# Hybrid encoder block on one core: block 0 in two tiles, and the second expert choice moved beside block 1's projections

## The reference

```python
proj = h @ w_in                                   # GDN q,k,v,z,a,b | FoX q,k,v,f | two merge gates
y_a = _gdn_branch(...)                            # conv + SiLU, L2 norm, chunked delta rule, gated RMS norm
y_b = _fox_branch(...)                            # 8 heads of causal attention with forget gates
mix = jax.nn.sigmoid(gate_a) * y_a + jax.nn.sigmoid(gate_b) * y_b
h = _layernorm(DEEPNORM_ALPHA * h + mix @ w_o, ln1_g, ln1_b)
...
top_s, top_i = lax.top_k(scores, PEER_TOPK)       # per head: 2 x 128 scores, 16 best of each
best_s, best_pos = lax.top_k(cand.reshape(...), PEER_TOPK)
u = jnp.take(u_tab, e_blk, axis=0)                # 8 x 16 = 128 rows of 1024 for every token
act = jax.nn.gelu(jnp.einsum('td,tkd->tk', h_blk, u), approximate=False) * g_blk
vv = jnp.take(v_tab, e_blk, axis=0)
y = jnp.einsum('tk,tkd->td', act, vv)
h = _layernorm(DEEPNORM_ALPHA * h + y, ln2_g, ln2_b)
```

## Time and profile before

| | |
|---|---|
| median of 3 executions | 3630.0 us (3629.85 to 3632.14) |
| the profiled execution | 3634.61 us |
| its span, first to last instruction | 3632.9 us |
| mean granted TensorE clock | 0.812 |
| busy: PE, DVE, POOL, ACT | 68%, 58%, 62%, 18% of the span |
| moved by DMA | 1290.18 MB, mean 355 GB/s |
| of it, expert rows | 1073.87 MB |
| chain that ended last | PE 25%, DMA 24%, POOL 17%, DVE 15%, issue 13% |

### The profile page before, as it was taken

How to read it: one execution, slowest core, us unless ns; L and a number is a source line. 1 busy time by engine, 2 the same in 40 slices (tenths; PEclk the granted TensorE clock), 3 DMA queues, 4 the chain that set the end, 5 groups by cost and what they waited for, 6 DMA issues and landing times.

```text
span 3632.9 us, 37417 instructions
## 1 busy us (share of the span) xinstructions
PE 2487.4 (68%) x12216; PEld 1529.5 (42%) x12216; DVE 2100.5 (58%) x4943; ACT 659.0 (18%) x1657; POOL 2243.1 (62%) x2093
## 2 busy tenths in 40 slices
PE   8888994676976876666977877667796730133355
PEld 6676772444744543433745543434563410000010
DVE  5133799885468776455359776455447569744400
ACT  3331321332013212322003312321101000000000
POOL 1000477677537766677566766677766667777774
PEclk9999997887998988877988988867798875555676
DMA  5214799899979999999999999999999999999997
GB/s 174 84 61 157 290 404 369 312 370 377 412 283 375 409 403 370 328 384 385 411 412 351 409 406 389 332 386 391 383 414 381 409 409 409 410 409 409 409 410 317
DMA packets 367626, 1290.18 MB, mean 355 GB/s; under 512 B 39596, under 2 KB 68148, under 8 KB 362308
## 3 DMA queue, kind: packets, MB, share of 16 engines
q0 software_dynamic: 294912, 1073.87, 75.8%
q1 hardware_dynamic: 66760, 201.33, 14.9%
q10 hardware_dynamic: 5760, 12.59, 0.9%
HBM read 1274.65 MB, written 12.98 MB: 354 GB/s over the span
## 4 chain that ended last, share of the span: by engine, by line
PE 25%; DMA 24%; POOL 17%; DVE 15%; issue 13%; ACT 3%; DVEq 2%; SPq 0%; ACTq 0%; POOLq 0%
DMA ring<-in_ev,idxT 11%; PE banks L1507 10%; POOL ring L788 9%; DVE ring L1203 7%; POOL ring L774 7%; DMA ring<-in_eu,eidx 5%; PE banks L1517 5%; PE banks L1496 4%; DMA arena<-in_eu,eidx 4%; PE banks L1780 2%; DMA arena<-in_ev,idxT 2%; PE banks L1636 1%; POOL arena L788 1%; DMA arena<-d_rows 1%; PE banks L1558 1%
## 5 line engine op out<-in xcount | busy, mean ns | idle before, releaser
L774 POOL DMA_INDIRECT ring<-in_eu,eidx x938 | 1058.4, 1128 | 898.6 <-DVE eidx L1466 436.4
L788 POOL DMA_INDIRECT ring<-in_ev,idxT x894 | 971.0, 1086 | 368.1 <-issue 251.7
L1203 DVE CUSTOM_DVE_ANT_0 ring<-ring,h_cur 128x1024 f32<-128x1024 f32 x768 | 906.7, 1222 | 188.6 <-DMA ring<-in_eu,eidx 186.3
L1496 PE MATMUL banks<-ring,wide 128*32 128x512 f32 x3576 | 642.0, 800 | 509.5 <-DMA ring<-in_ev,idxT 436.8
L1507 PE MATMUL banks<-arena,wslot 128*128 128x256 f32 (+1 forms) x3248 | 751.1, 389 | 16.4 <-DMA wslot<-in_w_pq 9.5
L1507 PEld LDWEIGHTS banks<-arena,wslot 128*128 128x128 f32 (+1 forms) x3248 | 624.5, 195 | 176.2 <-issue 68.8
L1496 PEld LDWEIGHTS banks<-ring,wide 128*32 128x32 f32 x3576 | 120.4, 131 | 839.1 <-DMA ring<-in_ev,idxT 437.2
L1203 DVE CUSTOM_DVE_ANT_0 ring<-ring,banks 128x1024 f32<-128x1024 f32 x170 | 205.7, 1221 | 109.1 <-DMA ring<-in_eu,eidx 105.8
L1517 PE MATMUL banks<-arena 128*128 128x128 f32 x1408 | 210.7, 307 | 35.6 <-ACT arena L957 33.6
L1517 PEld LDWEIGHTS banks<-arena 128*128 128x128 f32 x1408 | 198.9, 219 | 78.4 <-ACT arena L957 43.5
L1496 PE MATMUL banks<-arena,wide 128*32 128x512 f32 x520 | 143.7, 900 | 112.0 <-DMA ring<-in_ev,idxT 60.6
(11 more groups left out here) (294 smaller groups left out, 2844.0 us busy)
## 6 DMA issues: line engine op xcount, KB each, us to landing
wslot<-in_w_pq SPq DMA_DIRECT2D x64, 576.0 KB, 8.2
wslot<-in_w_mix SPq DMA_DIRECT2D x24, 1536.0 KB, 10.6
wslot<-in_w_qkv SPq DMA_DIRECT2D x48, 512.0 KB, 7.4
wslot<-in_w_fqk SPq DMA_DIRECT2D x32, 512.0 KB, 8.2
wslot<-in_w_out SPq DMA_DIRECT2D x8, 2048.0 KB, 10.8
ring<-in_eu,eidx POOLq DMA_INDIRECT x938, 13.6
ring<-in_ev,idxT POOLq DMA_INDIRECT x894
wslot<-in_w_z SPq DMA_DIRECT2D x16, 512.0 KB, 7.0
```

What stands on the lines that cost most here:

```text
L774: pool.indirect_dma_start(out=place(UPOS[k]), out_offset=None, in_=eu, in_offset=bass.IndirectOffsetOnAxis(ap=eidx[:, n % (2 * TT), c // T ...
L788: pool.indirect_dma_start(out=place(VPOS[k]), out_offset=None, in_=ev, in_offset=bass.IndirectOffsetOnAxis(ap=idxT[:, n % (2 * TT), t:t + ...
L1203: dve.tensor_tensor_reduce(out=row, in0=row, in1=h_cur[:, n % 3, :] if n < NT - TT else hp[n % 2], scale=1.0, scalar=0.0, op0=ALU.mult, op ...
L1496: last = pe.matmul(BY[k][32 * j:32 * j + 32, :], wide32[:, at:at + 32], place(VPOS[4 * q + j])[:, k * 512:(k + 1) * 512], start=(m == 0), ...
```

## The change

- Block 0 goes tile by tile. First come the projections, chunk 0 and the gates; then tile 0's own 9 attention units, `ot`, 8 `mix` on 128 tokens, 2 `wo`, `ln` and its choice. Chunk 1 and tile 1's attention and merge (`delta_of(1) + attend_of(1) + merge_of(1)`) are spread among the first choice.
- The second choice comes after that, with block 1's projections spread among it; its scores are computed anew for tile 1 (queries by 128x128 matmuls; `kept` is gone).
- Block 1's delta rule has no other units beside it.
- `mo`, `w_out` and `w_pq` weights are fetched once per tile of block 0. The second tile's two halves of `w_out` share one half of `wslot`, so the second is fetched when the first has been used.
- SP issues the decays of chunk 1 at the first level of chunk 0 instead of after the last, in all blocks.
- In block 0, DVE adds the identity at each level; the identity matmul and ACT's copy are gone there.
- Four ring slots hold block 0's data until the first choice is done (`LENT`). `SECOND, VSECOND` become 208, 96.

What `pace()` asks for at the borders of the stages (U items / V items done):

| by the unit | before | changed |
|---|---|---|
| `idx 0` of block 0 (end of the first choice) | 106 / 0 | 106 / 0 |
| `idx 1` of block 0 (end of the second choice) | 160 / 64 | 177 / 68 |
| block 1's attention begins | 162 / 64 | 209 / 96 |
| block 1's merge begins | 211 / 92 | 255 / 116 |
| block 1's first head is chosen | 256 / 120 | 256 / 120 |
| block 2's merge begins | 461 / 324 | 485 / 348 |
| block 3's layer norm | 768 / 632 | 768 / 628 |

```diff
-SECOND, VSECOND = 160, 64
+LENT = [11, 12, 15, 16]
+SECOND, VSECOND = 208, 96
...
+def delta_of(c):
+    return [("prod", c)] + [("lev", LEVELS * c + l) for l in range(LEVELS)] + [("wu", c), ("ws", c), ("o", c), ("og", c)]
...
+def attend_of(t):
+    return [u for m in range(FH + 1) for u in (("att", (FH + 1) * t + m), ("ato", (FH + 1) * t + m))] + [("ot", t)]
...
+def merge_of(t):
+    return [("mix", PH * t + i) for i in range(8)] + [("wo", TT * t + nh) for nh in range(2)] + [("ln", t)]
...
-    beside = [u for u in PROJECT if u not in early] + [u for m in range(MA + 1) for u in (("att", m), ("ato", m))]
+    beside = [u for u in PROJECT if u not in early]
...
+        if kind == "lev" and i or kind in ("ws", "o", "og"):
+            units += [("gt", 0, m), ("gt", 0, m + 1)]
+            m += 2
+    units += [(kind, 0, i) for kind, i in attend_of(0) + merge_of(0)]
+    units += [(kind, 0, i) for kind, i in spaced(PASSES[0], delta_of(1) + attend_of(1) + merge_of(1), 2)]
     for b in range(NB):
         if b:
-            late, done = PASSES[1][:-1] if b == 1 else [], 0
-            for n, (kind, i) in enumerate(DELTA[:-1]):
...
+            units += [(kind, b, i) for kind, i in DELTA[:-1] + ATTEND[:1] + DELTA[-1:] + ATTEND[1:] + MERGE]
         after = PROJECT if b + 1 < NB else []
-        choose = CHOOSE if b else PASSES[0]
+        choose = CHOOSE if b else PASSES[1]
...
     if name in ("mix", "wo"):
-        return n % 2, 0, 24 * P if name == "mix" else 32 * P
+        return 1 if n >= 2 and name == "wo" else n % 2, 0, 24 * P if name == "mix" else 32 * P
...
             def lev(b, cl):
+                c, l = divmod(cl, LEVELS)
+                if l == 0 and c + 1 < TT:
+                    sp.wait_ge(g["exps"], TT * b + c + 1)
+                    sp.wait_ge(g["qk"], TT * b + c + 1)
+                    gates(TT * b + c + 1)
...
-            def wu(b, c):
-                if c + 1 < TT:
-                    sp.wait_ge(g["wu"], TT * b + c + 1)
-                    gates(TT * b + c + 1)
...
+            def first_block(t):
+                W, KH, VH = P * (t + 1), KH0[t], VH0[t]
...
+                else:
+                    sp.wait_ge(g["S"], TT)
+                    sp.wait_ge(g["oT"], TT)
+                for i in range(FH // 2):
+                    row = FOX0 + 2 * i
+                    sp.dma_start(KH[0:FD, i, :, 0:W], d_fk[i, :, 0:W].rearrange("(j p) w -> p j w", j=2)).then_inc(s_att[i % 2], 16)
...
             def wo(b, i):
                 nh, tt = divmod(i, TT)
+                if b == 0:
+                    sp.wait_ge(s_nat, i + 1)
...
+                    elif i == 2:
+                        fetch("wo", 3)
...
+                if n == 1:
+                    dve.wait_ge(s_hTe, 1)
+                    dve.wait_ge(s_h1st, 16)
...
+                if b == 0:
+                    dve.wait_ge(g["lp"], n * LEVELS + l + 1)
+                    dve.tensor_tensor(Pm, ident[:, None, :].to_broadcast([P, GH, P]),
+                                      B[4][:, :].rearrange("p (a b) -> p a b", a=GH), ALU.add).then_inc(g["lpe"], 1)
...
-                pe.matmul(B[4][:, :], ident[:, :], ident[:, None, :].to_broadcast([P, GH, P]), start=True, stop=False)
+                if b:
+                    pe.matmul(B[4][:, :], ident[:, :], ident[:, None, :].to_broadcast([P, GH, P]), start=True, stop=False)
```

More of the change, by code:

```diff
@@ L53, with spaced @@
 CHOOSE = [u for i in range(PH) for u in (("top", 2 * i), ("top", 2 * i + 1), ("cand", i), ("sel", i))] + [("idx", 0)]
+def delta_of(c):
[4 more added lines that the diff above has]
+    return [("mix", PH * t + i) for i in range(8)] + [("wo", TT * t + nh) for nh in range(2)] + [("ln", t)]
+def spaced(main, beside, ahead):
+    out, done = [], 0
+    for n, u in enumerate(main):
+        out.append(u)
+        upto = min(len(beside), max(0, (n + 1 - ahead) * len(beside) // (len(main) - 2 * ahead)))
+        out += beside[done:upto]
+        done = max(done, upto)
+    return out + beside[done:]
 def order():
@@ L212, in slots @@
         held[n] = p
-    return slot, before, wide
+    return slot, before, wide, full
 WEIGHED = [s - 1 for s in BEGUN]
-SLOT, BEFORE, WIDE = slots()
+SLOT, BEFORE, WIDE, FULL = slots()
 PLACED = UNITS.index(("idx", NB - 1, 0)) + 1
@@ L674, in wo @@
                 nh, tt = divmod(i, TT)
+                if b == 0:
+                    sp.wait_ge(s_nat, i + 1)
+                    if i == 0:
+                        for n in range(3):
+                            fetch("pq", n)
+                    elif i == 1:
+                        for n in range(4):
+                            fetch("mo", PH + n)
+                    elif i == 2:
+                        fetch("wo", 3)
+                    else:
+                        for item in range(4):
+                            fetch(*PITEMS[item])
+                    return
                 if tt == TT - 1:
@@ L1651, in wu @@
                 pe.wait_ge(g["kbg"], n + 1)
-                if b == 0 and c == TT - 1:
+                if b == 0 and c == 0:
                     pe.wait_ge(s_sga[0], 3)
@@ new lines, in att0, with ato0 @@
+                if last_n is not None:
+                    r = last_n % 2
+                    pe.wait_ge(s_ex[r], last_n // 2 + 1)
+                    pe.wait_ge(s_Oe, last_n)
+                    for k in range(t + 1):
+                        last = pe.transpose(TB0[t][:, k * P:(k + 1) * P], SX0[t][:, r, k * P:(k + 1) * P], ident[:, :])
+                    last.then_inc(s_T, 1)
+            def ato0(u):
+                t = u // (FH + 1)
+                n = step(0, u)[1]
+                if n is not None:
+                    i, j, _ = head_of(0, n)
+                    pe.wait_ge(s_Te, n + 1)
+                    for k in range(t + 1):
+                        last = pe.matmul(TB0[t][:, 0:FD], PT0[t][:, k, :], VH0[t][:, i, k, FD * j:FD * (j + 1)],
+                                         start=(k == 0), stop=(k == t))
+                    last.then_inc(s_O, 1)
@@ L1772, in wo @@
                 nh, tt = divmod(i, TT)
+                if b == 0:
+                    t, nh = divmod(i, TT)
+                    for j in range(2):
+                        pe.wait_ge(s_mix[j], 4 * (t + 1))
+                    arrived(b, "wo", i)
+                    pe.wait_ge(s_natev[nh], 2 + t)
+                    w = item("wo", i, KB)
+                    for k in range(KB):
+                        last = pe.matmul(B[4 + nh][:, :], MIXT[t][:, k, :], w[:, k, :], start=(k == 0), stop=(k == KB - 1))
+                    last.then_inc(s_nat, 1)
+                    return
                 if i == 0:
                     for j in range(2):
-                        pe.wait_ge(s_mix[j], 4 * (b + 1))
+                        pe.wait_ge(s_mix[j], 4 * (b + 2))
                 arrived(b, "wo", nh)
```

433 lines of the change are left out of this document (297 added, 136 removed).

## The result

The changed kernel takes 3795.3 us (median of 5 runs, 3789.4 to 3805.2) where the kernel before takes 3632.1 beside it (5 runs). The ratio is 1.0443, with an interval of 1.0421 to 1.0465: slower, by 163 us. Predicted were 3765 us and a range of 3670 to 3830. The profiled execution took 3805.2 us, its span is 3803.5; the forecast made against the profiled time was 3772.

What follows compares the result with a forecast made beforehand. PE was taken to bound the kernel before the first gather and DMA most stages after; stages summed to 1235 us against 1083.7, taken as +145, then -8: 3772 us profiled, 3765 median, range 3670 to 3830.

Steps and rivals of the forecast that it cites:

- The sum up to block 1's first gather: All stages up to block 1's first chosen head: 1235 us against 1083.7, 151 us later, of which 145 was taken.
- A: Start to the first gather: 324 us where 394.6 stood, a gain of 70, between 60 and 85.
- B: First choice, with tile 1's work beside it: 289 us against 197.9, ends 244 and 310; DMA cannot fill it.
- C: Second choice with block 1's projections: set by DMA, 245 us, ends 232 and 265.
- rival 3: Second choice: POOL's issue bounds it at 2.29 us per gather, 73 us more, time 3838; chance 0.08.
- D: Block 1's delta rule alone: a chain of 125 us, ends 105 and 140.
- E to G: Block 1's attention 92 us, merge to first query 128, then to the first head 32.
- rival 1: DMA bounds every stage, so only bytes and the earlier start count: 3629 or about 3600 us, not slower; chance 0.12.
- rival 2: Better overlap in first choice (250 us) and lone delta rule (115), both late waits won: 3700 to 3720 us; chance 0.25.
- The sum behind it: All after block 1's first head is chosen: decays' gain against a dry spell, tail the same, net -8 us.
- the dry spell: Block 2's `wo` to the next choice: items done sooner leave it without gathers, costing 10 to 20 us.
- up to 28 us come back: Delta rules of blocks 2 and 3: earlier decays remove waits of 14.17 and 14.56 us in stages with idle DMA.

Runs made afterwards that it cites:

- the second group: Runs on the quick chip: the changed kernel, 3804.0 us, and the same with SECOND, VSECOND = 160, 64, 3749.6 us, beside the kernel before, 3630.3 us.

## Why the prediction was right, and where not

**The sum up to block 1's first gather** held: 133 us later, where 151 was worked out and 145 taken. Part of that is luck, since its terms were off by -10, -22, +7, +12 and -6 us, and these cancel in part.
- A, to the first gather: 314 against 324 forecast. The gain is 81, not 70. From the merge on, PE's pieces came as said: the merge 31 to 16 us, the output projection 27.70 to 14.20.
- B, the first choice: 267 against 289. DVE was busy for 201 us, not the 229 summed: this is the term that was off. It did 98 U items there and not 106, which is 9 us; the rest isn't split. What DVE was to stand came as summed, 66 us against 60. The waits were there: 18.9 us for the output weight against 22 by the landing time of the earlier trace rows, 14.1 for the levels against 18. By the Trainium skill's page "DMA: Bandwidth & Descriptors", section "Anatomy of one DMA — SWDGE (gpsimd) path", the estimate was 14; that section is about transfers that POOL issues, while SP issues these, and the measured value lies between the two. The wait for tile 1's keys, put at "a few us", was 20.4.
- C, the second choice with the projections: 252 against 245, at DMA share 1.01 as forecast. POOL was busy for 177.60 us with 152 gathers, 1.17 each, so rival 3 (2.29 each) did not come. The earlier trace rows call DVE idle beside the gather of 0.94 us at 414.10; it was not, it ran short sorting operations there (0.09 to 0.69 us), and U items of 1.22 us beside the gather of 1.99. So what goes with the longer gathers is that kind of DVE work.
- D, the delta rule alone: 137.5 against 125. C + D is 390 where 370 was forecast and 201.7 stood: the largest loss, as predicted, and the thick delta rules show its kind.
- E to G, attention to the first head: 246 against 252.
B, C and D together are 657 us, forecast 659, where rival 1 needed 515. By the bytes that did move in them (75, 99 and 41 MB at 409 GB/s) it would have been 527, so rival 1 is out by either count. Rival 2 (B 250, D 115) did not come either.

**The sum behind it failed**: -8 forecast, +37.6 measured. The mis-sized term is "the new pace does block 2's items sooner and stands dry from its `wo` to the next choice, which costs 10 to 20". I took the dry spell for a small thing at one place. Idle DMA time, as (1 - share) x length, adds up behind 1216.67 to 36.0 us in block 2's merge, 6.7 in its choice, 4.7 in block 3's delta rule and 7.8 in its merge, 55 in all; in the kernel before the delta rules' 11.1 and 7.8 are all there is. The difference, 36 us, is nearly the whole 37.6. (In the second profile of the changed kernel, its quickest run of that group, the stretch is only 17.6 us longer than before, with the same share of 0.81 in block 2's merge.) With the old pace 8 us are left (three lines of 0.97 and 0.99), and the stretch behind the gather is 2529.5 us instead of 2586.8 and 2566.8 in the changed kernel's two profiles: the pace costs 37 to 57 us, not 10 to 20. Without it the stretch is 20 us shorter than the kernel before's 2549.2, 15 of it in two delta rules (below), and the new pace took that gain away. The items that were done too early had made block 2's delta rule DMA-bound (197.9 us with 137 gathers, against 159.2 with 98), and its merge, where a chain of PE runs at its own length anyway (189.4 us with 73 gathers, 193.8 with 113 in the kernel before), then had little to carry. The merge before, and what waited for rows in block 2's delta rule after (50.0 and 27.3 us, where the kernel before had 2.8 and 5.6):

```profile
1703.87:1897.70 193.83, 164.50 (x758) 106.44 (x757) 83.76 (x150) 17.02 (x39) 125.84 (x113) 0.90 1.02 406
```
```profile
DVE ring L1369 <- DMA ring<-in_eu,eidx: 50.0, 24, 5.3
PE banks L1708 <- DMA ring<-in_ev,idxT: 27.3, 7, 15.4
```

The second term there, "up to 28 us come back" for the decays, was over-sized too. The waits did go: no wait for `d_rows` stands in the chain any more. But in the changed kernel block 3's delta rule is as long as before (155.6 and 155.1 us). Its DMA share rose from 0.95 to 0.97, and PE's weight loads wait there 11.3 us for V rows, against 0.9 before and 0.8 with the old pace, which nearly makes up for the wait that was taken out. At 152.1 and 147.3 with the old pace the two were worth 15 us, by idle DMA time at most 19, and not 28.

So of the 174 us lost in the second group some 119 (3749.6 against 3630.3) belong to the order of the work with its extra weights, the decays' gain taken off, and some 54 to two numbers of the pace. That the change cost time was foreseen for the right reason, and a third of it came from a term that had been put at 10 to 20 us. The median ended 30 us above the forecast because the first sum was 12 too high and the second 45 too low; so part of that nearness, too, is luck.

What stays open: why 22 more gathers in block 1's choice take over 50 us on the slower chip (372 to 385 us against 307 to 318 with the old pace), where they took some 30 on the quick one (329 and 332 against 302). On the slower kind 132.7 MB moved there in 371.7 us and 118.5 in 317.6; at the latter's 373 GB/s the bytes account for 38 of the 54 us, and the rest is open. PE's waits at its V matmuls are longer there, but those traces don't show when a row landed. Whether the waits of the first choice (39 us for keys and output weight) could be had back wasn't tried, nor was the second choice beside the delta rule in the new order.

## What to carry to other kernels

Before taking a piece of work out from beside another to start it earlier, add up what each will take alone: here two stages of 202 us together became 390, for 81 us won at the start. A plan that fixes how much of a load may be done by which point should reach that limit just when the point comes; sooner, it crowds one stage and starves the next, and the price is the idle share of DMA summed over all stages, not the one gap one sees. A wait that was removed in a stage held by transfers was worth no more here than they stood idle there. And read a DMA share against what gathers alone reach on the same chip: 0.88 was no room where that is 0.96.

## What the hardware showed that was not expected

- Different chips served the same gathers at 410 and 370 GB/s in like stretches of the tail, and the kernel before took 3630 and 3786 us. The price of the pace went with it: in the changed kernel from 1.5% (1.0486 against 1.0331) to 3.8% (with the late decays in it), and 5.0 and 5.1% in the kernel before. It isn't that the same idle time costs more. Added up as above over the whole stretch behind block 1's first gather, in twelve equal windows, the new pace brought 40 and 49 us more of idle DMA time on the quick chip (stretch 37 and 57 us longer), but 88 to 134 us more on the slower kind (115 to 156 longer). Why more stands idle there isn't shown.
- In the first choice the granted TensorE clock fell to 0.68, where it had been 0.94 in the earlier trace rows: a part of the stretch was at the lower level, 1.2 of 2.4 GHz, while PE was busy for 126 of 267 us with waits between. Sixteen matmuls of the output projection took 10.05 and 9.41 us there, and 14.20 us per 32 at 264.64, before that stretch. No term of the sum had this in it.
